# Mixture-of-experts stage: rows gathered three experts ahead, a weight's low part made on GpSimd

## The reference, cut to what matters

```
scores = sigmoid(xf @ router_w);  idx = top 8 of (scores + bias)
gates  = scores[idx] / sum * 2.5
for each of 64 experts e, for its tokens h = xf[tok]:
    y = (silu(h @ w1[e]) * (h @ w3[e])) @ w2[e]          # 1024 -> 256 -> 1024
    routed[tok] += y * gate
x = layer_norm(ALPHA * x + routed + shared(xf))
```

## Time and profile before

| | us |
|---|---|
| runs of the kernel | 2452.0 median of 3 (2451.42 to 2452.56) |
| profiled execution | 2446.4 |
| its span | 2444.6 |
| expert stages: output scaling of the first to that of the last expert | 486.9 to 1154.4 and 1694.7 to 2358.3 |

### The profile page before, as it was taken

How to read it: one execution, slowest core, us unless ns; L and a number is a source line. 1 busy time by engine, 2 the same in 40 slices (tenths; PEclk the granted TensorE clock), 3 DMA queues, 4 the chain that set the end, 5 groups by cost and what they waited for, 6 DMA issues and landing times. The chain is left out here.

```text
span 2444.6 us, 33315 instructions
## 1 busy us (share of the span) xinstructions
PE 2183.8 (89%) x10840; PEld 1569.7 (64%) x10840; DVE 1647.0 (67%) x2772; ACT 1366.1 (56%) x1754; POOL 429.0 (18%) x310
## 2 busy tenths in 40 slices
PE   6999999699999998998679999996999999999956
PEld 5688756476666666676266886565666666666632
DVE  2583323588888887886545833246888888888847
ACT  3534631377777776776034356215777777777731
POOL 0001000122222222222000010002222232223210
PEclk9999999899999999999789999998999999999978
DMA  6213030599999998996731220307999999999965
GB/s 194 75 44 147 1 140 20 173 339 348 346 346 340 345 345 337 341 340 248 292 85 52 70 121 1 146 14 262 336 344 341 349 341 338 344 338 350 349 239 241
DMA packets 140839, 575.79 MB, mean 236 GB/s; under 512 B 40228, under 2 KB 65060, under 8 KB 88792
## 3 DMA queue, kind: packets, MB, share of 16 engines
q1 hardware_dynamic: 95704, 507.54, 55.4%
q0 software_dynamic: 45056, 67.22, 8.8%
HBM read 551.00 MB, written 61.37 MB: 250 GB/s over the span
## 5 line engine op out<-in xcount | busy, mean ns | idle before, releaser
L1318 DVE TENSOR_TENSOR w_lo<-w,w_hi 128x2048 fp32r<-128x2048 f32 x256 | 587.0, 2293 | 128.1 <-ACT w_hi L1389 128.1
L1389 ACT CAST w_hi<-w 128x2048 fp32r<-128x2048 f32 x256 | 490.5, 1917 | 111.3 <-PE ps_up L1235 69.0
L1233 PE MATMUL ps_up<-w_hi,rowsT_hi 128*100 128x512 f32 x1024 | 421.9, 412 | 6.7 <-DVE rowsT_lo L1330 6.7
L1234 PE MATMUL ps_up<-w_lo,rowsT_hi 128*100 128x512 f32 x1024 | 405.7, 396 | 0.0
L1235 PE MATMUL ps_up<-w_hi,rowsT_lo 128*100 128x512 f32 x1024 | 403.9, 394 | 0.0
L1170 POOL DMA_INDIRECT rows<-x_rows,index x128 | 245.3, 1916 | 336.9 <-DVE index L1303 296.5
L1179 POOL DMA_INDIRECT y_rows<-y,y_index x128 | 136.8, 1068 | 940.6 <-DVE index L1303 889.9
L1218 PE MATMUL ps_t<-square,rows 100*128 100x100 f32 x1024 | 143.7, 285 | 109.9 <-DMA rows<-x_rows,index 109.3
L1218 PEld LDWEIGHTS ps_t<-square,rows 100*128 100x128 f32 x1024 | 128.0, 204 | 154.4 <-DMA rows<-x_rows,index 150.4
L1323 DVE TENSOR_TENSOR w_lo<-w,w_hi 128x2048 fp32r<-128x2048 f32 x96 | 219.4, 2285 | 2.8 <-ACT w_hi L1396 2.8
L1258 PE MATMUL ps_y<-w_hi,hiddenT_hi 128*100 128x512 f32 x512 | 216.0, 422 | 4.1 <-DVE hiddenT_lo L1337 4.1
(11 more groups left out here) (223 smaller groups left out, 3710.3 us busy)
## 6 DMA issues: line engine op xcount, KB each, us to landing
w<-exp_w SPq DMA_DIRECT2D x356, 1024.0 KB, 12.2
w_first<-exp_w SPq DMA_DIRECT2D x34, 1024.0 KB, 12.2
got<-y_rows SPq DMA_DIRECT2D x8, 4096.0 KB, 13.6
wbuf<-w_in SPq DMA_DIRECT2D x16, 1024.0 KB, 5.6
w_out_sb<-w_out SPq DMA_DIRECT2D x2, 4096.0 KB, 19.2
bias<-bias_tiles SPq DMA_DIRECT2D x2, 2560.0 KB, 9.1
sh_w<-sh_w SPq DMA_DIRECT2D x4, 1024.0 KB, 9.1
x_rows<-x_sb SPq DMA_DIRECT2D x8, 512.0 KB, 2.6
```

The source lines that it names most:

```text
L1233: pe.matmul(ps_up[b][0:CAP], hi, w_hi, start=(k == 0), stop=False)
L1234: pe.matmul(ps_up[b][0:CAP], hi, w_lo, start=False, stop=False)
L1318: dve.tensor_tensor(w13_lo[:, :, k, :], w13[:, x.slot % 2, :, k, :], w13_hi[:, :, k, :].bitcast(F32), ALU.subtract).then_inc(S["up_lo_b" i ...
L1389: act.copy(w13_hi[:, :, k, :], w13[:, x.slot % 2, :, k, :]).then_inc(S["up_hi_b" if half else "up_hi_a"], 1)
```

## The change

The row buffer gets four slots instead of two (`rows` [P, SLOTS, D], semaphores `rows0_in` to `rows3_in`), and lists, picks and gathers run three experts ahead instead of two. `index` and `gate` get eight slots (LAP = 8), the scatter reads its destinations from `index` itself, and `place`, `y_index` and `y_placed` go. A lap has eight steps, so that the loop runs over six laps. `dn_lo` moves from VectorE's program to the end of GpSimd's step, and also waits for `down_made(x-2)`. SyncE's first load waits for the third gather's turn. To make room, the routing part reuses temporaries: `left` and `place` share `sel`, `gate` shares `e`, the shared expert's product is written over `act_out`, and the unused output of the squares is bfloat16.

```diff
-        junk = T("junk3", [P, D])
+        junk = T("junk3", [P, D], BF16)
...
-        shT = T("shT", [P, 2, SEQ])
-        e, s, sel, left, mask, gate = (T(n, [P, NT, NE]) for n in ("e", "s", "sel", "left", "picked", "gate_raw"))
-        place = T("place", [P, NT, NE])
+        e, s, sel, mask = (T(n, [P, NT, NE]) for n in ("e", "s", "sel", "picked"))
+        left, gate, place = sel, e, sel
...
+LAP = 8
 SLOTS = 4
...
-                sp.wait_ge(S["dma_turns"], 2)
+                sp.wait_ge(S["dma_turns"], 3)
...
                 def gather(x):
-                    b = x.slot % 2
                     pool.wait_ge(S["index_ready"], x.n + 1)
+                    if x.has(-SLOTS):
+                        pool.wait_ge(S["rows_turned"], x.n - SLOTS + 1)
+                    pool.sem_inc(S["dma_turns"], 1)
+                    pool.indirect_dma_start(rows[0:CAP, x.slot, :], None, d["x1_rows"],
+                                            bass.IndirectOffsetOnAxis(ap=index[0:CAP, x.step, 0:1], axis=0),
+                                            bounds_check=SEQ - 1, oob_is_err=False).then_inc(S[f"rows{x.slot}_in"], 16)
+
+                def dn_lo(x):
+
+                    pool.wait_ge(S["dn_hi"], x.n + 1)
                     if x.has(-2):
-                        pool.wait_ge(S["rows_turned"], x.n - 1)
+                        pool.wait_ge(S["down_made"], x.n - 1)
+                    pool.tensor_tensor(w2_lo[:, x.slot % 2], w2[x.slot], w2_hi[:, x.slot % 2].bitcast(F32), ALU.subtract
+                                       ).then_inc(S["dn_lo"], 1)
...
-                gather(Turn(0, 0))
-                gather(Turn(0, 1))
+                for k in range(3):
+                    gather(Turn(0, k))
 
                 def step(x):
                     if x.has(-2):
                         put(x + -2)
-                    if x.has(2):
-                        gather(x + 2)
+                    if x.has(3):
+                        gather(x + 3)
+                    dn_lo(x)
                 _laps(pool, step)
...
                 def step(x):
-                    if x.has(2):
-                        pick(x + 2)
+                    if x.has(3):
+                        pick(x + 3)
...
                 def indices(x):
-                    b = x.slot % 2
                     dve.wait_ge(S["picked_made"], x.n + 1)
-                    if x.has(-SLOTS):
-                        dve.wait_ge(S["rows_turned"], x.n - SLOTS + 1)
-                        dve.wait_ge(S["y_made"], x.n - SLOTS + 1)
-                        dve.wait_ge(S["y_placed"], x.n - SLOTS + 1)
-                    dve.tensor_reduce(gate[0:CAP, x.slot:x.slot + 1], ps_p[0:CAP, GATES:GATES + 3], AX.X, ALU.add)
+                    if x.has(-LAP):
+                        dve.wait_ge(S[f"y{x.slot}_out"], 16 * (x + -LAP).times(SLOTS))
+                    dve.tensor_reduce(gate[0:CAP, x.step:x.step + 1], ps_p[0:CAP, GATES:GATES + 3], AX.X, ALU.add)
...
                 def step(x):
+                    if x.has(4):
+                        hots(x + 4)
                     if x.has(3):
-                        hots(x + 3)
-                    if x.has(2):
-                        indices(x + 2)
+                        indices(x + 3)
...
-                    dn_lo(x)
-                    if x.has(-1):
-                        place(x + -1)
```

More of the change, by code:

```diff
@@ L1046, in _mix_and_route, with __init__, times @@
         _restart(nc, S)
+LAP = 8
 SLOTS = 4
 class Turn:
-    def __init__(self, lap, slot):
-        self.lap, self.slot = lap, slot
-        self.n = lap * SLOTS + slot
+    def __init__(self, lap, step):
+        self.lap, self.step = lap, step
+        self.n = lap * LAP + step
+        self.slot = step % SLOTS
         self.known = isinstance(lap, int)
     def __add__(self, k):
-        s = self.slot + k
-        return Turn(self.lap + s // SLOTS, s % SLOTS)
+        s = self.step + k
+        return Turn(self.lap + s // LAP, s % LAP)
     def has(self, k):
         return not self.known or 0 <= self.n + k < NE
+    def times(self, slots):
+        return self.lap * (LAP // slots) + self.step // slots + 1
 def _laps(eng, step):
-    for s in range(SLOTS):
+    for s in range(LAP):
         step(Turn(0, s))
-    with eng.Fori(1, NE // SLOTS - 1) as lap:
-        for s in range(SLOTS):
+    with eng.Fori(1, NE // LAP - 1) as lap:
+        for s in range(LAP):
             step(Turn(lap, s))
-    for s in range(SLOTS):
-        step(Turn(NE // SLOTS - 1, s))
+    for s in range(LAP):
+        step(Turn(NE // LAP - 1, s))
+LAST = Turn(NE // LAP - 1, LAP - 1)
 def _expert_weights(d):
@@ L1114, in _experts @@
         hot = T("hot", [P, 2, NT, CAP], BF16)
[L1115 to L1117 removed]
+        index = T("index", [P, LAP, 2], I32)
+        gate = T("gate", [P, LAP])
         rows = sb["rows"]
@@ L1212, in turn_rows @@
                 def turn_rows(x):
-                    b = x.slot % 2
-                    pe.wait_ge(S[f"rows{b}_in"], 16 * (x.lap * (SLOTS // 2) + x.slot // 2 + 1))
+                    pe.wait_ge(S[f"rows{x.slot}_in"], 16 * x.times(SLOTS))
                     if x.has(-1):
@@ L1261, in down @@
                     mm.then_inc(S["down_made"], 1)
-                pick(Turn(0, 0))
-                pick(Turn(0, 1))
+                for k in range(3):
+                    pick(Turn(0, k))
                 turn_rows(Turn(0, 0))
                 def step(x):
-                    if x.has(2):
-                        pick(x + 2)
+                    if x.has(3):
+                        pick(x + 3)
                     up(x, 0)
@@ L1278, in _ @@
                 _laps(pe, step)
-                last = Turn(NE // SLOTS - 1, SLOTS - 1)
-                turn_hidden(last)
-                down(last)
+                turn_hidden(LAST)
+                down(LAST)
             @block.vector
@@ L1338, in hidden_lo @@
                                       ).then_inc(S["hidden_lo"], 1)
-                def place(x):
-                    dve.wait_ge(S["index_ready"], x.n + 1)
-                    if x.has(-SLOTS):
-                        dve.wait_ge(S[f"y{x.slot}_out"], 16 * x.lap)
-                    dve.tensor_copy(y_index[0:CAP, x.slot:x.slot + 1], index[0:CAP, x.slot, 1:2]).then_inc(S["y_placed"], 1)
                 hots(Turn(0, 0))
@@ L1367, in step @@
                         up_lo(x + 1, 1)
-                    dn_lo(x)
-                    if x.has(-1):
-                        place(x + -1)
                 _laps(dve, step)
-                last = Turn(NE // SLOTS - 1, SLOTS - 1)
-                hidden_lo(last)
-                place(last)
+                hidden_lo(LAST)
                 dve.wait_ge(S["hot_ready"], NE)
@@ L1392, in dn_hi @@
                     if x.has(-1):
-                        act.wait_ge(S[f"dn{x.slot}_in"], 16 * (x.lap + 1 if x.slot else x.lap))
+                        act.wait_ge(S[f"dn{x.slot}_in"], 16 * (x.times(SLOTS) if x.slot else x.times(SLOTS) - 1))
                     if x.has(-2):
@@ L1442, in _ @@
                 _laps(act, step)
-                last = Turn(NE // SLOTS - 1, SLOTS - 1)
-                hidden_hi(last)
-                scaled(last)
+                hidden_hi(LAST)
+                scaled(LAST)
         _restart(nc, S)
@@ L1550, in trunk @@
                     sb |= {"w13": left("w13", [P, 2, 2, KD, FF]), "w2_first": left("w2_first", [P, 2, D]),
-                           "rows": left("rows", [P, 2, D])}
+                           "rows": left("rows", [P, SLOTS, D])}
                     _mix_and_route(nc, d, sb, l)
```

38 lines of the change are left out of this document (15 added, 23 removed).

## The result

The changed kernel takes 2485.6 us (median of 4 runs, 2483.4 to 2486.8) beside 2451.7 for the kernel before (4 runs, 2449.2 to 2452.6): ratio 1.014, 95% interval 1.0124 to 1.0156. The forecast was 2415. Times are medians of all runs; the ratios leave out the one run in which the granted clock was low throughout (0.716; 2825.85 us, one of four of h0 in experiment 5).

A forecast was written before the change was run, and what follows sets the result against it. Late gathered rows were taken to lengthen the expert steps, with every engine nearly full. 2446.4 - 37 (122 steps at 10.4 instead of 10.70) - 4 + 4 = 2409.4, plus 5.6 to the median: 2415 us; 8-in-10 range 2382 to 2530.

The forecast's parts named there:

- the line that put half a directly under GpSimd's subtraction: Next expert's half a (up weights' low part, VectorE) is held by GpSimd's subtraction until 6.69 us after half b's start.
- rival 1: GpSimd's gather loses the dead heat against VectorE's half b: steps of 11.7 us, about 2574 us if all lose; chance 0.29.
- Row waits go: TensorE's steady-step waits for gathered rows, 1.03 us per step, vanish with gathers three ahead; it then needs 9.5 to 9.6.
- The 1.2 us between this and 10.70 is what more gather lead can win: Expert steps average 10.70 us, TensorE's own work is 9.5; issuing gathers earlier could win the 1.2 us between.
- GpSimd's subtraction, 4.55 us alone and 4.40 after b: Third weight's low part, moved to GpSimd: 4.55 us alone, ending 4.40 us after VectorE's half b when held by it.
- Long GpSimd reads hold VectorE: GpSimd's long SBUF read blocks VectorE instructions with two SBUF inputs: half a lengthened to 3 us or more.
- rival 2: VectorE is not held by GpSimd, shown by half a staying at 2.29: steps 10.15 us, about 2385 us; chance 0.11.
- The cycle of 10.3 us: Expert step set by VectorE and GpSimd excluding one another: 10.19 us, with 0.1 for two hand-overs 10.3 us.
- Transfers allow 10.15 to 10.55 us: Expert step's 3.67 MB by DMA, best rate 348 GB/s extrapolated to 362: 10.15 to 10.55 us; 0.1 added, step 10.4.
- rival 3: Transfers already bind the expert steps at 342 GB/s: step stays 10.7 us, time 2452; chance 0.11, including a balance of both.
- Start and end, −4 and +4: Over both expert stages: first rows arrive earlier, -4 us in all; the longer last low part costs +4 us.

The follow-up runs named there:

- h0: Kernel before the change, with half of w2's (third weight's) load left out from the fifth expert on: 2343.2 us, ratio 0.9564.
- experiment 5: Half of w2's load left out in the kernel before (2343.2 us), the changed kernel (2485.7) and the changed kernel with the low part back on VectorE (2315.9).
- Experiment 2: Changed kernel with the comparisons' source stored as 25 runs of 4 at pitch 5, to be read through one port: 2454.3 us, ratio 1.0035.
- experiment 1: Changed kernel with the low part of the third weight made on VectorE again, gathers still three ahead: 2438.4 us, ratio 0.9973.
- h5: Changed kernel with one-port comparisons, the fourth just ahead of half b, and half of w2's load left out from the fifth expert: 2402.7 us, ratio 0.9808.
- experiment 6: Changed kernel with one-port comparisons and half of w2's load left out from the fifth expert on: 2428.7 us, ratio 0.9928.
- experiment 8: Changed kernel with one-port comparisons, the fourth just ahead of half b: 2442.5 us with all bytes, 2402.7 with half of w2's load left out.
- e8: Changed kernel with one-port comparisons, the fourth moved to just ahead of half b, all bytes moved: 2442.5 us, ratio 0.9974.
- h1: Changed kernel with half of w2's load left out from the fifth expert on: 2485.7 us, ratio 1.0154.
- experiments 2 and 4: Changed kernel, either with comparisons read through one port (2454.3 us, 1.0035) or with them moved behind the product for hidden (2444.8 us, 0.9989).

## Why the prediction was wrong

The step that failed is the line that put half a directly under GpSimd's subtraction: "Half a of the next expert, which could start about 5.6 us after b's start (as 906.97 against 901.36), is held until 2.29 + 4.40 = 6.69". Between b and a VectorE has the comparisons, and it is they that are held, with everything in order behind them. The sum took them as done beside GpSimd's work, at nothing and without a reason given; 0.84 us came on top (0.51 of comparisons, 0.33 of lists and `hidden_lo`). With it and the 0.06 us that GpSimd took longer, 10.19 becomes 11.09; measured are 11.08. The prediction looked for port users only among instructions with two SBUF inputs. The comparison has one, bf16, SBUF to SBUF. The Trainium skill (SBUF — State Buffer, section SBUF: two separate sides) names as holders of the shared ports also VectorE instructions in a two-port mode, and (VectorE: DVE Perf Modes, section Mode 2×_2P) gives the conditions of it: one source, both ends in SBUF, outer dimensions both even or equal. Experiment 2 agrees: with 25 runs in the source and 100 elements in the destination the hold of 4.6 us is gone.

In time: 122 steps at 11.05 instead of 10.4 us are 79 us more than forecast; starts and ends took 5 us less, and from the profiled execution to the median it was 1.1 instead of 5.6. That is the way from 2415 to 2485.6. That the measured time lies in the range for 8 in 10 (2382 to 2530) is luck: its upper end was there for rival 1, which did not come.

Term by term:

- *Row waits go*: right. They were not what bounded the step, though: experiments 1 and 5 show that the kernel before stood at the transfers' limit. "The 1.2 us between this and 10.70 is what more gather lead can win" is the second failed step. With all bytes the lead won nothing in the steps (10.74 and 10.70) and 0.3% at the starts and ends (experiment 1); with fewer bytes 27 us, half of them outside the steps.
- *GpSimd's subtraction, 4.55 us alone and 4.40 after b*: 4.61 (experiment 6, at 905.36) and 4.46. Right.
- *Long GpSimd reads hold VectorE* (rival 2 said no): right, but the victims were the comparisons; half a is held in their place (2.7 to 3.2 us, 4.3 after a lost heat) once they are out of the way. Rival 2 is out. The sign given for it, half a at 2.29, would have misled: half a stayed at 2.28 because the comparisons ahead of it had waited the hold out.
- *The cycle of 10.3 us*: exists, once the comparisons use one port and the heat is decided: 10.37 in h5, of which 0.2 is the comparison put in. The 0.1 for hand-overs was not needed.
- *The dead heat* (rival 1): did not occur in the kernel after. The scatter came 0.64 us ahead of half a instead of 0.3 us behind its start, and the gather was held by a, not by b (2.40 us, 0.95 past a's end), which cost nothing, since GpSimd then waited 0.8 us for ScalarE. It is real in experiment 6, on both sides of 0.02 us. A lost one costs 1.1 us a step (10.2 to 11.3), not 1.4.
- *Transfers allow 10.15 to 10.55 us*: wrong for this kernel, and rival 3 (0.11) right about the bound of the kernel before, though not about the time after. The 348 GB/s of the best 105 us, at a share of 0.96, had been stretched to 362 at 1.0; experiment 8 has 343 at 0.98 and 349 at 0.97, and over a whole stage 340, as before. Neither the best 105 us nor the 8% of idle engine time in the earlier trace rows could be had in every step. So even the forecast cycle, allowed by the port in e8, gives 2442.5 us and not 2415. The Trainium skill (DMA: Bandwidth & Descriptors, section Specifications) has some 358 GB/s for one core's share of the memory; no stage here passed 341, and whether that share is what bounds a core that runs alone, as here, no run shows.
- *Start and end, −4 and +4*: −5.0 together instead of 0 (−3.8, −1.4, +0.2). Each was larger than forecast: the two starts gave 3.8 and 6.5 us (up to the first scaling; from the first layer's last scaling to the second's first), the two ends cost 5.1 and 1.1 (from the scaling of expert 61 to that of 63), and 0.9 were won behind them. The jumps of the longer loop cost nothing: h1's steps average 11.07 and 11.08 us, and those at the laps' ends differ from the others by 0.2 us at most.

The port explains the loss: h1 is unchanged without the bytes, experiments 2 and 4 bring 1.014 down to 1.0035 and 0.9989 by dealing with the comparisons alone. Of the 37 us of gain that were forecast, no version with all bytes had more than 8.4 (experiment 1). The fastest version that moves all bytes is experiment 1 (0.9973), level with e8 (0.9974) within their intervals. Not settled: why the mix of 8 KB weight pieces and 4 KB rows averages 340 to 341 GB/s over a stage; no run that moves all bytes changed the sizes of the pieces or the number of buffers.

## What to carry to other kernels

Before work goes to GpSimd, list every VectorE instruction that can stand beside it, by port: two SBUF inputs, and one input with SBUF at both ends in a fast mode, however short. A 0.2 us comparison can be held for 4.6 us, and all that is queued behind it starts only then: here that was 0.84 us of a step, where the whole change was to win 0.3. Moving such an instruction, or giving its source an odd outer dimension that the destination hasn't, took one edit here. And before a wait for rows at a DMA share above 0.9 is called latency, try the kernel with fewer bytes: the row waits went in experiment 1 and the steps stayed.

## What the hardware showed unexpectedly

- A comparison of 128x100 bf16 (0.24 us) is held for up to 4.62 us by GpSimd's 4.6 us read. Through one port it is never held and four cost 0.82 instead of 0.70 us.
- The hold is mutual: half a, 2.28 us alone, takes 3.2 or 4.3 us behind a GpSimd subtraction and ends some 2.2 us after it, nearly as if it had started only then. In the trace before, VectorE had lost no more than 0.06 us (2.35 for 2.29).
- With the gather 0.02 us ahead of half b by the profile, either of the two can win; start times don't show which, and it swings a step by 1.1 us (experiment 6).
- The DMA share is no measure of what is left: stages of three kernels average 340 to 341 GB/s at shares of 0.92, 0.95 and 0.96. With a seventh fewer bytes the kernel before moves only 310, at 0.86.
